# Three gate passes of 48, 32 and 48 sub-tiles instead of four of 32, in a two-layer encoder trunk with product-key experts

## The chip, the cores and the metric

The kernel runs on one core of one Trainium2 chip. A core has TensorE (PE; its weight loads are written PEld), VectorE (DVE), ScalarE (ACT), GpSimd (POOL) and SyncE (SP, which issues the DMAs). The metric is the device time of one execution in microseconds. Before the change it is 2258.52 us, the median of 3 runs (2255.5 to 2259.55).

## The reference

Two layers over 256 tokens of width 1024, all in float32. A layer is a norm, one input projection, sliding-window attention beside an RWKV-7 recurrence, an output projection, then the expert stage, then a gated embedding. The change touches only the expert stage:

```
def _peer(h, wq, keys, u_tab, v_tab):
    q = (h @ wq).reshape(B, S, PEER_HEADS, 2, PEER_HALF)
    sc = jnp.einsum('bshcd,cnd->bshcn', q, keys)          # 128 scores on each of two axes
    top_v, top_i = lax.top_k(sc, 16)
    cand = top_v[..., 0, :, None] + top_v[..., 1, None, :]
    best_v, best_c = lax.top_k(cand.reshape(..., 256), 16)
    expert = i1 * 128 + i2                                 # i1, i2 of the 16 best pairs
    gate = softmax(best_v)
    ...
        u = jnp.take(u_tab, ex, axis=0)
        act = gelu(einsum('thkd,td->thk', u, hx)) * gx
        out = einsum('thk,thkd->td', act, jnp.take(v_tab, ex, axis=0))
```

There are 16384 experts, and a token uses 128 slots of them (8 heads, 16 each). The kernel gathers nothing. It computes the hidden value of every expert for every token, multiplies it with a gate that is zero for unused experts, and multiplies the result with the whole v table.

## The kernel before

Experts are cut by their second index i2 into 128 sub-tiles of 128 experts (i1 is the partition). All products of float32 matrices are done as three products of a high and a low part: ACT copies a tile into `high` (L648), DVE or POOL subtracts it to give `low` (L1083, L435), and TensorE adds high x high, high x low and low x high.

For one sub-tile e there are four kinds of work on TensorE:
- `hidden(e)` (L1624): 24 products of 256 columns, u tile times the tokens; ACT then puts gelu of it into `GA` (L652).
- `spread(g)` (L1636): for a group of 8 tokens, the gates of one pass. For each token it multiplies `hot1` (slots x i1, one-hot) with `hot2` (slots x i2 of the pass; three bfloat16 parts of the gate, each on the one-hot of i2) into one PSUM bank: 3 products of 32 columns a token, 24 a group. The three parts add up in PSUM.
- `spend(s)` (L1647): 12 products of 512 columns, gated activations of sub-tile s times its v tile, summed in PSUM banks 0 to 3.

DVE makes the one-hots of a group in `one_hots` (is_i2 L1146, hot1 L1149, hot2 L1153), after ACT has repeated the slot numbers (`repeat`, L678). DVE multiplies gates into GA in `apply_gates` (L1161), straight from PSUM. ACT and DVE split the gated activations in `split_w` (WH L669, WL L1166).

A pass gives the gates of 32 sub-tiles for all 256 tokens, as 32 groups; there are four passes in a layer. GA holds 64 sub-tiles (`HELD`), so sub-tile 64 + s goes where sub-tile s was. The order of a layer's expert stage is written out by hand and is the same on every engine:
- First part: `hidden` 0 to 39, with POOL making the low parts, while DVE does the top-k.
- Second part: `hidden` 40 to 63 with all 32 spreads of pass 0 between them (DVE makes the low parts from here on).
- Joint part: 64 steps of spread, hidden(64 + s), spend(s): passes 1 and 2.
- Fourth part: 32 steps of spread, spend(64 + s): pass 3.
- Last part: 32 steps of spend(96 + s).

The engines meet only by semaphores. A spread waits for its one-hots (`hots_made`) and for the gates two groups back to be applied (`gated`), since there are two PSUM banks for gates. DVE waits for ACT's repeats (`repeated`) and, before applying, for the spread (`spread_ps`). The tables arrive as slabs of 1 MB of two tiles, through a ring of four, each asked for by SP when DVE or POOL has used the old one.

## Time and profile before

| what | value |
|---|---|
| median of 3 runs | 2258.52 us |
| profiled execution, its own time | 2252.36 us |
| its span | 2250.6 us |
| PE busy | 2162.7 us (96%), 21816 matmuls |
| PEld busy | 1939.7 us (86%) |
| DVE busy | 1588.3 us (71%) |
| ACT busy | 1092.5 us (49%) |
| POOL busy | 336.4 us (15%) |
| granted TensorE clock, mean | 0.987 |
| of the matmuls, L1636 (spread) | 6144 of 128x32, bfloat16 |

The profiled execution is 6.2 us under the median of the runs, so differences are made against its own time and then carried to the median. A busy span of a matmul covers its latency, which overlaps with the next; what one costs in a stream is read from the starts of neighbouring rows. The same is true, to a lesser degree, of DVE: a following instruction often starts before the end of the one before it.

### The profile page before, as it was taken

Reading aid. Unit: us, or ns where it says so; the run is one execution under the profiler, and the core shown is the slowest. Engines: PE = TensorE matmul, PEld = TensorE weight load, DVE = VectorE, ACT = ScalarE, POOL = GpSimd, SP = SyncE. Lnnn points to the kernel's source line nnn. Section 1 sums busy time; section 2 is a strip of 40 time slices with the busy share of each in tenths; the row PEclk is TensorE's granted clock in tenths of the full one; section 3 lists DMA queues with packets and bytes.
Section 4 is the critical chain, followed back from the end, with each engine's and each line's share of the span. In section 5 each row is a group of like instructions: output and inputs, shape, how many; then the busy total and the mean of one; then the engine's idle time right before and its main releaser. Section 6 shows DMA issues by size and latency. Waiting matters only on the chain.

```text
span 2250.6 us, 55219 instructions
## 1 busy us (share of the span) xinstructions
PE 2162.7 (96%) x21816; PEld 1939.7 (86%) x21816; DVE 1588.3 (71%) x3080; ACT 1092.5 (49%) x1881; POOL 336.4 (15%) x166
## 2 busy tenths in 40 slices
PE   8889999999999999999998899999999999999997
PEld 8878999988888888788788789999888888887885
DVE  6645896876666667975576458968766666679755
ACT  5534455444444444444454344554444444444443
POOL 0022696000000000000000237950000000000000
PEclk9999999999999999999999999999999999999999
DMA  6212344434444444445342134443344444444451
GB/s 255 94 41 102 143 171 174 142 131 168 167 164 165 164 165 165 149 168 187 134 149 93 41 125 142 181 167 135 131 168 168 168 168 168 166 153 150 167 200 70
DMA packets 46618, 335.04 MB, mean 149 GB/s; under 512 B 5168, under 2 KB 5296, under 8 KB 6320
## 3 DMA queue, kind: packets, MB, share of 16 engines
q1 hardware_dynamic: 46512, 333.61, 41.2%
q8 instruction: 69, 1.13, 0.2%
q14 instruction: 37, 0.30, 0.0%
HBM read 332.54 MB, written 1.05 MB: 148 GB/s over the span
## 4 chain that ended last, share of the span: by engine, by line
PE 80%; issue 6%; POOL 6%; DVE 5%; ACT 1%; DMA 1%; POOLq 0%; SPq 0%; DVEq 0%; ACTq 0%
PE PS L1647 32%; PE PS L1624 23%; PE PS L1309 8%; PE PS L1636 6%; POOL low L435 5%; PE PS L1325 3%; PE PS L1489 1%; DVE low L1083 1%; PE PS L1527 1%; PE PS L1538 1%; DVE hot L1153 1%; DVE hot L1149 1%; DMA ring<-in_w_slabs 1%; ACT high L459 0%; PE PS L1357 0%
## 5 line engine op out<-in xcount | busy, mean ns | idle before, releaser
L648 ACT CAST high<-ring 128x1024 fp32r<-128x1024 f32 x512 | 535.6, 1048 | 602.1 <-PE PS L1624 443.2
L1624 PE MATMUL PS<-hTh,high 128*128 128x256 f32 x2048 | 594.8, 290 | 13.0 <-ACT GA L652 11.0
L1624 PE MATMUL PS<-hTh,low 128*128 128x256 f32 x2048 | 578.4, 282 | 0.0
L1624 PE MATMUL PS<-hTl,high 128*128 128x256 f32 x2048 | 577.0, 282 | 0.0
L1083 DVE TENSOR_TENSOR low<-ring,high 128x1024 fp32r<-128x1024 f32 x432 | 514.8, 1217 | 0.8 <-ACT high L648 0.6
L1624 PEld LDWEIGHTS PS<-hTh,high 128*128 128x128 f32 x2048 | 387.1, 189 | 17.7 <-ACT GA L652 9.7
L1624 PEld LDWEIGHTS PS<-hTl,high 128*128 128x128 f32 x2048 | 387.6, 189 | 0.0
L1624 PEld LDWEIGHTS PS<-hTh,low 128*128 128x128 f32 x2048 | 387.3, 189 | 0.0
L1647 PE MATMUL PS<-high,WH 128*128 128x512 f32 x1024 | 323.6, 397 | 0.0
L1647 PE MATMUL PS<-low,WH 128*128 128x512 f32 x1024 | 317.9, 392 | 0.0
L1647 PE MATMUL PS<-high,WL 128*128 128x512 f32 x1024 | 316.4, 390 | 0.0
L1146 DVE TENSOR_TENSOR is_i<-iota_half,repeats 128x256 bf16<-128x256 bf16 x256 | 73.8, 288 | 257.1 <-ACT repeats L678 253.0
L395 POOL TENSOR_SCALAR stat<-stat 128x1 f32<-128x1 f32 x14 | 5.1, 367 | 1609.8 <-ACT xn L468 1609.8
L435 POOL TENSOR_TENSOR low<-ring,high 128x1024 fp32r<-128x1024 f32 x80 | 226.4, 2867 | 32.7 <-ACT high L648 32.7
L1647 PEld LDWEIGHTS PS<-high,WL 128*128 128x128 f32 x1024 | 192.2, 188 | 42.9
L1647 PEld LDWEIGHTS PS<-low,WH 128*128 128x128 f32 x1024 | 192.2, 188 | 42.8
L1636 PEld LDWEIGHTS PS<-hot,hot 128*128 128x128 bf16 x6144 | 169.9, 96 | 60.1 <-issue 54.1
L1647 PEld LDWEIGHTS PS<-high,WH 128*128 128x128 f32 x1024 | 178.9, 188 | 26.5
L1636 PE MATMUL PS<-hot,hot 128*128 128x32 bf16 x6144 | 194.0, 177 | 7.6 <-DVE hot L1153 7.6
L669 ACT CAST WH<-GA 128x256 fp32r (+1 forms) x256 | 102.8, 402 | 201.5 <-PE PS L1647 191.0
L1309 PE MATMUL PS<-hTh,high 128*128 128x256 f32 x592 | 172.7, 292 | 2.9 <-DVE hTl L835 2.9
L1149 DVE TENSOR_TENSOR hot<-iota_half,repeats 128x1024 bf16<-128x1024 bf16 x256 | 174.9, 683 | 0.0
(251 smaller groups left out, 2980.1 us busy)
## 6 DMA issues: line engine op xcount, KB each, us to landing
ring<-in_peer_slabs SPq DMA_DIRECT2D x256, 1024.0 KB, 4.8
ring<-in_w_slabs SPq DMA_DIRECT2D x58, 1024.0 KB, 4.8
xres<-in_x SPq DMA_DIRECT2D x2, 512.0 KB, 4.3
out<-obuf SPq DMA_DIRECT2D x2, 512.0 KB, 2.6
cst<-in_consts SPq DMA_DIRECT2D x1, 680.0 KB, 10.1
praw<-in_p_t SPq DMA_DIRECT2D x1, 512.0 KB, 14.8
gfin<-in_g_final SPq DMA_DIRECT2D x1, 512.0 KB, 5.6
vec<-in_vecs SPq DMA_DIRECT2D x1, 356.0 KB, 7.0
```

The source lines that it names most:

```text
L435: pool.tensor_tensor(low[:, b], ring[:, place, half * D:(half + 1) * D], high[:, b].bitcast(F32), ALU.subtract).then_inc(low_pool, 1)
L648: act.copy(high[:, (c0[L] + j) % DEEP], ring[:, place, half * D:(half + 1) * D]).then_inc(part_hi, 1)
L669: act.copy(WH[:, j % 2:j % 2 + 1], GA[:, bass.ds(place, 1)]).then_inc(w_hi, 1)
L1083: dve.tensor_tensor(low[:, b], ring[:, place, half * D:(half + 1) * D], high[:, b].bitcast(F32), ALU.subtract).then_inc(low_dve, 1)
L1146: dve.tensor_tensor(is_i2[:, b].rearrange("p t (a c) -> p t a c", c=REP), iotas[:, QT // REP * chunk:QT // REP * (chunk + 1)].unsqueeze(1) ...
L1149: dve.tensor_tensor(hot1[:, b].rearrange("p t (a c) -> p t a c", c=REP), iotas.unsqueeze(1).broadcast_to([P, GROUP, NSUB // REP, REP]), re ...
L1153: dve.tensor_tensor(hot2[:, b].rearrange("p q t (a c) -> p q t a c", c=REP), is_i2[:, b].rearrange("p t (a c) -> p t a c", c=REP).unsqueez ...
L1309: ins = mm(dst, w[:, b, ks], h[:, k], start=n == 0, stop=n == 3 * KT - 1)
L1325: ins = mm(PS[:, bank0 + 2 * tb + s], h[:, k, tb * P:(tb + 1) * P], w[:, b, s * 512:(s + 1) * 512], start=first and k == 0 and c == 0, sto ...
L1624: ins = mm(PS[:, 6 + j % 2, 0:SEQ], u[:, b, ks], h[:, k], start=n == 0, stop=n == 3 * KT - 1)
L1636: ins = mm(PS[:, 4 + b, t * QT:(t + 1) * QT], hot1[:, b, t], hot2[:, b, part, t], start=part == 0, stop=part == 2)
L1647: ins = mm(PS[:, 2 * tb + s], w[:, j % 2, tb * P:(tb + 1) * P], v[:, b, s * 512:(s + 1) * 512], start=False, stop=False, skip_group_check= ...
```

## The change

Passes are 48, 32 and 48 sub-tiles wide. GA holds 80 sub-tiles. The order is now: `hidden` 0 to 47 with POOL; `hidden` 48 to 79, each followed by one spread of pass 0; 32 steps of spread (pass 1), hidden(80 + s), spend(s); 16 steps of hidden and spend alone; 32 steps of spread (pass 2) and spend(48 + s); 48 steps of spend. In passes 0 and 2 a token still takes three products, of 48 columns. In pass 1 it takes two: one of 64 columns, the first two gate parts side by side, and one of 32 columns, the third part, added onto the second half. The two halves are added by DVE (`sum_gates`, a reduction from PSUM into the new tile `gate_sum`), and `apply_gates` then reads `gate_sum`.

```
-NQ = 4
-QT = NSUB // NQ
-HELD = 2 * QT
+STARTS, WIDTHS = (0, 48, 80), (48, 32, 48)
+NQ, WIDEST = len(WIDTHS), max(WIDTHS)
+HELD = WIDTHS[0] + WIDTHS[1]
+JOINT = NSUB - HELD
-A_FIRST, A_SECOND, A_TOP, A_LOOP = 16, 32, 36, 40
+A_FIRST, A_SECOND, A_TOP, A_LOOP = 16, 32, 44, 48
+        gate_sum = place("gate_sum", 16016, [WIDTHS[1], GROUP])
...
                 def apply_gates(g, group, b, chunk):
+                    start, width = place_of(STARTS[chunk]), WIDTHS[chunk]
+                    acts = GA[:, start:start + width, bass.ds(GROUP * group, GROUP)]
+                    if chunk == 1:
+                        dve.wait_ge(gates_summed, NGROUPS * (L - 1) + 1 + g)
+                        dve.tensor_tensor(acts, acts, gate_sum[:], ALU.mult).then_inc(gated, 1)
+                    else:
+                        dve.wait_ge(spread_ps, g0 + 1 + g)
+                        dve.tensor_tensor(acts, acts, PS[:, 4 + b, 0:GROUP * width].rearrange("p (t i) -> p i t", t=GROUP), ALU.mult).then_inc(gated, 1)
+
+                def sum_gates(g, b):
                     dve.wait_ge(spread_ps, g0 + 1 + g)
-                    acts = GA[:, chunk % 2 * QT:chunk % 2 * QT + QT, bass.ds(GROUP * group, GROUP)]
-                    dve.tensor_tensor(acts, acts, PS[:, 4 + b, 0:GROUP * QT].rearrange("p (t i) -> p i t", t=GROUP), ALU.mult).then_inc(gated, 1)
+                    dve.tensor_reduce(gate_sum[:], PS[:, 4 + b].rearrange("p (t q i) -> p i t q", t=GROUP, q=2), AX.X, ALU.add).then_inc(gates_summed, 1)
...
                 for e in range(A_LOOP, HELD):
                     if e < HELD - 2:
                         split_u(e + 2)
-                    for g in spreads_after(e):
-                        first_chunk(g, g % 2, g == NGROUPS - 1)
+                    first_chunk(e - A_LOOP, e % 2, e == HELD - 1)
...
                 def step(s, j, group, chunk, last=False):
                     one_hots(s + (NGROUPS + 1), (j + 1) % 2, chunk + last)
-                    split_uv(s + 1, j + 1)
+                    split_uv(s + 1, j + 1, 0)
+                    sum_gates(s + NGROUPS, j % 2)
+                    split_uv(s + 1, j + 1, 1)
                     apply_gates(s + NGROUPS, group, j % 2, chunk)
                     split_w(s + 1, s + 1, j + 1)
...
-                def spread(g, b):
+                def spread(g, b, chunk):
+                    width = WIDTHS[chunk]
...
                     for t in range(GROUP):
+                        if chunk == 1:
+                            at = 2 * t * width
+                            mm(PS[:, 4 + b, at:at + 2 * width], hot1[:, b, t], hot2[:, b, 0:2, t, 0:width], start=True, stop=False, skip_group_check=True)
+                            ins = mm(PS[:, 4 + b, at + width:at + 2 * width], hot1[:, b, t], hot2[:, b, 2, t, 0:width], start=False, stop=True, skip_group_check=True)
+                            continue
                         for part in range(3):
-                            ins = mm(PS[:, 4 + b, t * QT:(t + 1) * QT], hot1[:, b, t], hot2[:, b, part, t], start=part == 0, stop=part == 2)
+                            ins = mm(PS[:, 4 + b, t * width:(t + 1) * width], hot1[:, b, t], hot2[:, b, part, t, 0:width], start=part == 0, stop=part == 2)
...
-                with pe.Fori(0, HELD // 4) as i:
+                with pe.Fori(0, NGROUPS // 4) as i:
                     for j in range(4):
-                        spread(4 * i + (j + NGROUPS), j % 2)
+                        spread(4 * i + (j + NGROUPS), j % 2, 1)
                         hidden(4 * i + (j + HELD), j, 2 * j, second=True)
                         spend(4 * i + j, j, 2 * j + 1, low_dve, v0[L] + 2 + 2 * (4 * i + j))
-                with pe.Fori(HELD // 4, (HELD + QT) // 4) as i:
+                with pe.Fori(NGROUPS // 4, JOINT // 4) as i:
                     for j in range(4):
-                        spread(4 * i + (j + NGROUPS), j % 2)
-                        spend(4 * i + j, j, j, low_dve, v0[L] + (HELD + 1) + 4 * i + j)
+                        hidden(4 * i + (j + HELD), j, 2 * j, second=True)
+                        spend(4 * i + j, j, 2 * j + 1, low_dve, v0[L] + 2 + 2 * (4 * i + j))
+                with pe.Fori(JOINT // 4, (JOINT + NGROUPS) // 4) as i:
+                    for j in range(4):
+                        spread(4 * i + (j + 2 * NGROUPS - JOINT), j % 2, 2)
+                        spend(4 * i + j, j, j, low_dve, v0[L] + (JOINT + 1) + 4 * i + j)
```

What stands on TensorE at the start of a joint step (`spread`, then `hidden`), before:

```order
L1636 MATMUL PS<-hot_113,hot_112 128x32 x24
L1612 ISA
L1619 REGISTER_ALU
L1624 MATMUL PS<-hTh,high 128x256
L1624 MATMUL PS<-hTl,high 128x256
```

And now, the first two of the eight tokens:

```order
L1623 MATMUL PS<-hot_114,hot_113 128x64
L1624 MATMUL PS<-hot_114,hot_113 128x32
L1623 MATMUL PS<-hot_114,hot_113 128x64
L1624 MATMUL PS<-hot_114,hot_113 128x32
```

The block of 24 products has become one of 16, alternately of 64 and 32 columns; what follows it is as it was, under other line numbers.

What stands on DVE in a joint step (`step`), with the semaphores waited for, before:

```order
L1146 TENSOR_TENSOR is_i_114<-iota_half,repeats 128x256 [waits repeated]
L1149 TENSOR_TENSOR hot_112<-iota_half,repeats 128x1024
L1153 TENSOR_TENSOR hot_113<-is_i_114,repeats 128x768 [waits is_i2_made]
L1081 ISA
L1083 TENSOR_TENSOR low<-ring,high 128x1024 [waits part_hi]
L1081 REGISTER_ALU
L1083 TENSOR_TENSOR low<-ring,high 128x1024 [waits part_hi]
L1159 REGISTER_ALU
L1161 ISA [waits spread_ps]
L1161 TENSOR_TENSOR GA<-GA,PS 128x32x8
L1165 REGISTER_ALU
L1166 ISA [waits w_hi]
```

And now:

```order
L1125 TENSOR_TENSOR is_i_115<-iota_half,repeats 128x8x32 [waits repeated]
L1128 TENSOR_TENSOR hot_113<-iota_half,repeats 128x1024
L1132 TENSOR_TENSOR hot_114<-is_i_115,repeats 128x24x32 [waits is_i2_made]
L1059 ISA
L1061 TENSOR_TENSOR low<-ring,high 128x1024 [waits part_hi]
L1149 REGISTER_ALU
L1150 TENSOR_REDUCE gate_sum<-PS 128x256 [waits spread_ps]
L1061 TENSOR_TENSOR low<-ring,high 128x1024 [waits part_hi]
L1142 ISA [waits gates_summed]
L1142 TENSOR_TENSOR GA<-GA,gate_sum 128x32x8
L1155 ISA [waits w_hi]
```

The reduction stands between the two subtractions of the slab, the wait for the spread has moved to it, and the one-hots have lost their contiguous shape, since a pass of 32 is now written into tiles laid out for 48.

## Rows read from the trace of the kernel before

**Rows 1.** The page's part 4, the chain that ended last, by engine

```profile
PE 80%; issue 6%; POOL 6%; DVE 5%; ACT 1%; DMA 1%; POOLq 0%; SPq 0%; DVEq 0%; ACTq 0%
```

**Rows 2.** Windows: stretch, us, busy (count) of PE PEld DVE ACT POOL, clock, DMA, GB/s

```profile
389.30:477.10 87.80, 86.12 (x1250) 84.50 (x1249) 73.64 (x141) 40.44 (x76) 0.00 (x0) 1.00 0.39 132
477.10:489.90 12.80, 10.06 (x111) 9.18 (x110) 9.02 (x15) 4.06 (x8) 0.00 (x0) 0.73 0.36 127
480.53:481.20 0.67, 0.67 (x24) 0.67 (x24) 0.67 (x2) 0.40 (x1) 0.00 (x0) 0.50 0.00 0
489.90:886.80 396.90, 396.90 (x3782) 353.86 (x3782) 272.28 (x441) 190.88 (x316) 0.00 (x0) 1.00 0.46 165
886.80:998.00 111.20, 111.20 (x1154) 88.88 (x1154) 100.70 (x190) 54.39 (x96) 0.00 (x0) 1.00 0.42 151
998.00:1085.10 87.10, 87.10 (x386) 72.16 (x385) 51.01 (x64) 43.27 (x63) 0.00 (x0) 1.00 0.55 194
```

**Rows 3.** Timeline of TensorE, a joint step: start us, us, what, count

```profile
565.48 0.77 PE L1636 MATMUL PS<-hot,hot 128*128 128x32 bf16 x24
566.10 0.36 PE L1624 MATMUL PS<-hTh,high 128*128 128x256 f32 x1
569.03 0.63 PE L1647 MATMUL PS<-high,WH 128*128 128x512 f32 x2
```

**Rows 4.** Timeline of DVE, the same step; in brackets the idle time before

```profile
567.12 0.29 DVE L1146 TENSOR_TENSOR is_i<-iota_half,repeats 128x256 bf16<-128x256 bf16 x1 [1.92 <-ACT repeats L678]
567.33 0.68 DVE L1149 TENSOR_TENSOR hot<-iota_half,repeats 128x1024 bf16<-128x1024 bf16 x1
567.93 0.55 DVE L1153 TENSOR_TENSOR hot<-is_i,repeats 128x768 bf16<-128x768 bf16 x1
568.40 2.35 DVE L1083 TENSOR_TENSOR low<-ring,high 128x1024 fp32r<-128x1024 f32 x2
570.67 0.41 DVE L1161 TENSOR_TENSOR GA<-GA,PS 128x256 f32 x1
571.00 0.42 DVE L1166 TENSOR_TENSOR WL<-GA,WH 128x256 fp32r<-128x256 f32 x1
573.42 0.29 DVE L1146 TENSOR_TENSOR is_i<-iota_half,repeats 128x256 bf16<-128x256 bf16 x1 [2.00 <-ACT repeats L678]
```

**Rows 5.** Timeline of TensorE, end of the second part and first joint step

```profile
477.06 1.36 PE L1636 MATMUL PS<-hot,hot 128*128 128x32 bf16 x48
480.53 0.82 PE L1636 MATMUL PS<-hot,hot 128*128 128x32 bf16 x24 [2.10 <-DVE hot L1153]
481.99 0.58 PE L1624 MATMUL PS<-hTh,high 128*128 128x256 f32 x1 [0.64 <-DVE low L1083]
```

**Rows 6.** Timeline of TensorE, two spreads of the second part

```profile
408.96 0.77 PE L1636 MATMUL PS<-hot,hot 128*128 128x32 bf16 x24
412.50 0.77 PE L1636 MATMUL PS<-hot,hot 128*128 128x32 bf16 x24
```

**Rows 7.** Timeline of TensorE, a spread of the fourth part

```profile
928.46 0.77 PE L1636 MATMUL PS<-hot,hot 128*128 128x32 bf16 x24
```

**Rows 8.** Timeline of DVE, the fourth part

```profile
929.38 0.42 DVE L1161 TENSOR_TENSOR GA<-GA,PS 128x256 f32 x1 [0.31 <-PE PS L1636]
932.86 0.42 DVE L1161 TENSOR_TENSOR GA<-GA,PS 128x256 f32 x1 [0.31 <-PE PS L1636]
```

**Rows 9.** Chain of waits, pieces in order of time: start us, us, what

```profile
374.42 14.24 PE PS L1624 x120
...
995.22 89.91 PE PS L1647 x396
```

**Rows 10.** Groups by line: reductions on DVE, shapes, count, busy us, mean ns

```profile
L1124 DVE TENSOR_REDUCE slot<-picked 128x128 f32<-128x2048 f32 x8 | 18.3, 2286 | 0.3
...
L881 DVE TENSOR_REDUCE stat<-lg 128x8 f32<-128x1024 f32 x2 | 2.4, 1220 | 0.1
```

More of the change, by code:

```diff
@@ L213, in hybrid_encoder @@
         GA = place("GA", R, [HELD, SEQ])
[L214 to L219 removed]
+        WH = place("WH", R + 20480, [2, SEQ], F32R)
+        WL = place("WL", R + 20992, [2, SEQ], F32R)
+        hot1 = place("hot1", R + 21504, [2, GROUP, NSUB], BF16)
+        hot2 = place("hot2", R + 22528, [2, 3, GROUP, WIDEST], BF16)
+        is_i2 = place("is_i2", R + 23680, [2, GROUP, WIDEST], BF16)
+        decoded = place("decoded", R + 24064, [5, SEQ], BF16)
         gate_rest = place("gate_rest", R + 22208, [SEQ])
[L221 removed]
+        repeats = place("repeats", R + 24704, [2, 5, GROUP, REP], BF16)
         gate_T = place("gate_T", R + 19968, [SEQ])
@@ L741, in _ @@
+                with act.Fori(0, NGROUPS // RING - 1) as i:
                     for j in range(RING):
-                        step(i, j)
-                for j in range(RING):
-                    step(QT // RING - 1, j)
-                wrap = NGROUPS
-                with act.Fori(QT // RING, HELD // RING - 1) as i:
-                    for j in range(RING):
-                        step(i, j)
-                for s in range(HELD - RING, HELD):
+                        step(i, j, RING * i + j)
@@ L750, in _ @@
+                for s in range(NGROUPS - RING, JOINT - 2):
+                    step(s // RING, s % RING, s, s < NGROUPS)
+                for s in range(JOINT - 2, JOINT):
                     act.wait_ge(w_lo, NSUB * L + 1 + s)
-                    if s < HELD - 2:
-                        split_uv(s // RING, s % RING + 2, 0)
-                    else:
-                        act.wait_ge(part_used, c0[L] + C_UV + 2 * s + 1)
+                    act.wait_ge(part_used, c0[L] + C_UV + 2 * s + 1)
@@ L755, in _ @@
                     gelu(s, s)
[L756 to L771 removed]
+                    if s + 1 == STARTS[1]:
+                        act.wait_ge(gated, NGROUPS * (NQ * L + 2))
@@ L772, in late @@
+                    split_w(s + 1, s + 1, s + 1, C_UV + 2 * s - 1)
+                    for n in ((0,), (1, 2))[s - JOINT + 2]:
+                        split_vv(0, n)
+                def late(n, i, j, place, more=True, again=False):
+                    split_w(n, place, j + 1, C_VV - 1 + n)
                     if more:
@@ L1217, in _ @@
-                for s in range(HELD - RING, HELD):
-                    if s < HELD - 1:
-                        step(s, s % RING, s % QT, 2)
-                    else:
-                        one_hots(s + NGROUPS + 1, 0, 3)
-                        apply_gates(s + NGROUPS, s % QT, 1, 2)
-                        split_w(s + 1, 0, 0)
+                dve.wait_ge(ga_ready, NSUB * L + STARTS[2])
+                with dve.Fori(0, NGROUPS // RING - 1) as i:
+                    for j in range(RING):
+                        step(RING * i + j, j, RING * i + j, 1)
@@ L1224, in _, with last_chunk @@
+                for s in range(NGROUPS - RING, NGROUPS):
+                    step(s, s % RING, s, 1, s == NGROUPS - 1)
+                for s in range(NGROUPS, JOINT - 1):
+                    split_uv(s + 1, s % RING + 1, 0)
+                    split_uv(s + 1, s % RING + 1, 1)
+                    split_w(s + 1, s + 1, s + 1)
+                split_vv(0, 0)
+                split_w(JOINT, JOINT, JOINT)
                 dve.wait_ge(ga_ready, NSUB * (L + 1))
-                def last_chunk(n, j, last=False):
+                def last_chunk(n, j, place, last=False):
@@ L1665, in _ @@
                 ins.then_inc(slot_ps, 1)
-                for e in range(A_TOP, A_LOOP + 4):
-                    hidden(e, e, e, by_dve=e >= POOL_U)
-                    if e in (A_LOOP, A_LOOP + 2):
-                        spread(e // 2 - A_LOOP // 2, e // 2 % 2)
-                with pe.Fori(0, (HELD - A_LOOP - 4) // 4) as i:
-                    for j in range(4):
-                        hidden(4 * i + (j + A_LOOP + 4), j, j, by_dve=True)
-                        spread(6 * i + (2 + 3 * j // 2), 3 * j // 2 % 2)
-                        if j % 2:
-                            spread(6 * i + (2 + 3 * j // 2 + 1), (3 * j // 2 + 1) % 2)
@@ L1678, in _ @@
-                with pe.Fori(0, HELD // 4) as i:
+                for e in range(A_TOP, A_LOOP):
+                    hidden(e, e, e)
+                for e in range(A_LOOP, A_LOOP + 4):
+                    hidden(e, e, e, by_dve=True)
+                    spread(e - A_LOOP, e % 2, 0)
+                with pe.Fori(1, NGROUPS // 4) as i:
+                    for j in range(4):
+                        hidden(4 * i + (j + A_LOOP), j, j, by_dve=True)
+                        spread(4 * i + j, j % 2, 0)
@@ L1691, in _ @@
+                with pe.Fori((JOINT + NGROUPS) // 4, NSUB // 4) as i:
+                    for j in range(4):
+                        spend(4 * i + j, j, j, low_dve, v0[L] + (JOINT + 1) + 4 * i + j)
                 for n in range(4):
```

127 lines of the change are left out of this document (44 added, 83 removed).

## The prediction

> **What bounds the kernel now.** I read the chain of waits first: the reader is to see that PE holds 80% of it [rows 1]. Next the windows, cut at the borders of the parts of layer 0's expert stage: in the joint, the fourth and the last part PE is busy for the whole of the stretch at full granted clock, while DVE is busy for 69% of the first of them (272.28 of 396.90 us) and 91% of the second (100.70 of 111.20 us) [rows 2]. The DMAs are at about half their share. So one TensorE instruction taken out of those parts is time gained, as long as DVE keeps up. Then the timelines of one step, to price single pieces from the starts of rows.
>
> A joint step lasts 6.30 us, from one is_i2 to the next [rows 4]. On PE it is a spread, 0.62 us from its first product to the first of hidden; hidden, 2.93 us to the first of spend; and spend, the remaining 2.75 us [rows 3]. DVE works through its step from 567.12 to about 571.34 and then stands idle for 2.00 us until ACT's repeats arrive [rows 4]; ACT issues those behind its copy of the tile that spend has just freed, so the idle time is PE's lead. A step of the fourth part lasts 3.48 us (929.38 to 932.86), and there DVE has only 0.31 us to spare [rows 8].
>
> **The price of a product.** A block of 48 products of 32 columns takes 0.59 us more than a block of 24 (1.36 against 0.77), so one costs 0.59 us / 24 = 24.6 ns, say 25 ns, with its weight load [rows 3, 5]. At 2.4 GHz 32 columns are 13.3 ns, so more than 11 ns of it are not column time. The same block at half granted clock (0.50, 1.2 GHz) takes 0.82 us [rows 2, 5]; less the latency of about 0.2 us that is 27 ns a product, and 32 columns at 1.2 GHz are 26.7 ns. So at the low clock weight load and overhead hide wholly under the columns, and at the high clock something of 25 ns stands over them. I take it for a floor: 48 columns (20.0 ns) cost 25 ns still, so three products of 48 cost what three of 32 did; 64 columns (26.7 ns) stick out, 28 ns. Bounds: 25 ns for both from below, and from above in proportion to columns, 37.5 and 50 ns. I take the value near the lower end because the half-clock row is the only one of the same instruction at another ratio of column time to the rest.
>
> The Trainium skill, "TensorE: Matmul & The Clock Gate", sections "Wait — 56ns, not 53.3ns?" and "Back-to-back issue gap", states that start-to-start never falls below about 25 ns however small the product and gives about 60 cycles for 1 to 64 columns. The trace agrees at 32 columns (25 ns); no row shows 48 or 64. The same section's formula, columns / 2.4 + 2.5, would make 64 columns 29.2 ns, and the joint block 0.01 us longer than mine.
>
> **The change part by part, for one layer** (layer 0; the other has the same steps).
>
> *Second part.* Before, 87.8 us for 24 hiddens and 30 spreads [rows 2]. Now 8 of the hiddens fall in the first part, where five hiddens in a row take 14.24 us with the last one's latency, 2.84 us each [rows 9]: 22.7 us. POOL makes their low parts, but DVE is done with its top-k by then, as before. Then 32 hiddens with 31 spreads before the border. A hidden with one spread lasts 3.54 us (408.96 to 412.50) [rows 6]: 31 x 3.54 + 2.93 = 112.7 us. DVE has a wider job there. From neighbouring starts [rows 4], bfloat16 work costs 0.21 us for 256 elements, 0.60 for 1024 and 0.47 for 768, so about 0.52 ns an element more; the gate product takes 0.33 us for 256. At 48 wide is_i2 is 0.27, hot2 0.67, the gate product 0.47 us, with hot1 0.60 and one tile's subtraction 1.14 in all 3.15 us, under 3.54: hidden behind PE. After each apply DVE needs 2.7 us to have the next but one's one-hots ready, inside the step too. Sum 135.4 us, +47.6.
>
> *Border to the joint part.* Before, 12.8 us from the last hidden's end to the second joint spread, at a mean granted clock of 0.73 [rows 2]: two spreads at once, then PE idle for 2.10 and 0.64 us, then a whole hidden at half clock [rows 5]. Now one spread stands there and hots for the next are ready, since DVE made them a step earlier. hidden(80) waits for DVE: the gate product starts 0.92 us after the spread's first product (928.46, 929.38) [rows 7, 8], then 0.47 and one subtraction of 1.2 us, 2.65 us in all. With hidden 2.93 and spend 2.86 the second joint spread comes at 8.4 us if the clock holds, and 2.3 us later if it falls as before. PE's idle time shrinks from 2.7 to about 1.5 us but does not go. I take half of that loss: -3.2 (between -4.4 and -2).
>
> *Joint part.* Before, 63 more steps, 396.9 us [rows 2]. The spread is now 8 x (28 + 25) ns = 0.42 us instead of 0.60, so a step is 6.12 us. DVE gains a reduction of 512 elements to 256. The nearest rows are 2286 ns for 2048 elements and 1220 ns for 1024 [rows 10], 1.04 ns an element: 0.68 us; bounds 0.33 us (the pace of the 256-element gate product) and 1.22 us (the row of 1024). All of them fit in the idle 2.00 less the 0.18 us that the step gets shorter. ACT's repeats come as they did; queued behind the reduction are the v subtraction, the gate product and WL, and the earliest reader, the next hidden, needs none of them. So the reduction costs nothing; it would begin to from 1.8 us. 31 steps x 6.12 = 189.7, and 16 steps without a spread, 6.30 - 0.62 = 5.68: 90.9. Sum 280.6, -116.3.
>
> *Fourth part.* 32 steps before and now, at the same 25 ns a product. But DVE's work grows by 0.06 + 0.20 + 0.14 = 0.40 us against 0.31 us of idle time [rows 8], so it falls behind by 0.09 us a step, 2.9 us over 32. PE needs a gated activation late: WL of the next step is done about 1.7 us after the spread's start and read at 3.48 + 0.6, so 2.4 us of lag are free while it builds up. At the end sub-tile 80 needs the last gates of all, and there some of the lag is paid: +1.0 us (0 to 2.9).
>
> *Last part.* 48 spends instead of 32. 396 products take 89.91 us [rows 9], 0.227 us each, 12 a spend: 2.73 us. 16 x 2.73 = +43.7. One slab for two of them was met at 194 GB/s [rows 2] and the steps of 5.68 us ask no more.
>
> Sum a layer: 47.6 - 3.2 - 116.3 + 1.0 + 43.7 = -27.2 us; two layers -54.4. As a check, 32 spreads fewer at 0.62 and 32 shorter by 0.18 make -25.6, and the border -3.2, less the hand-overs. The profiled execution had 2252.4 us, so 2198.0 now (span 2196.2); against the median of 2258.5 that is **2204 us**.
>
> **Rivals.**
> - *Columns add to the overhead.* A float32 product of 256 columns costs 2.84 us / 24 = 118 ns [rows 9], 11.7 ns over its 106.7 ns of columns, and the 32-column product is 11.7 ns over its 13.3. If that sum holds between, 48 columns cost 31.7 ns and 64 cost 38.4. Against it: the half-clock row, where nothing is added, and that the 256-column row is float32, weights and all. It costs 24 x 6.7 = 0.16 us on 64 spreads and 8 x 10.4 = 0.08 us on 32, less the 1.0 of the fourth part, where PE would be slower than DVE: +12.0 a layer, **2228 us**.
> - *Cost in proportion to columns*, 37.5 and 50 ns: +0.30 us on 64 spreads, +0.18 on 32, -1: +23.8 a layer, **2252 us**. The half-clock row speaks for it only at the other clock.
> - *DVE becomes the bound, and the kernel slower.* The one-hots run at 0.52 ns an element, half the float32 pace of 1.04. If tiles written at widths of 48, or 32 in a tile laid out for 48, lose that pace, is_i2 takes 0.48 and hot2 1.28 us, and DVE's step is 3.97 us in the second part (PE 3.54) and 4.31 in the fourth (PE 3.48): 32 x 0.43 + 32 x 0.83 - 2.4 = +37.9, less the 1.0, +36.9 a layer, so 2204 + 74 = **2278 us**. It decides from 0.85 us a step, both parts together. For it: only that the shapes are new. Against: inner runs stay at 8 elements, and 256, 768 and 1024 elements lie on one line.
> - *The third product is not saved*, since the 64-column one costs as two: a case of the second rival.
>
> **How the numbers follow.** Forecast 0.62, added columns 0.23, in proportion 0.05, DVE 0.05, something unseen 0.05 (spread over all outcomes). The likeliest's own range is 2194 to 2213: 25 ns for 64 columns (-3), 27 for 48 (+6), the border's clock (-2 to +2), the fourth part's lag (-2 to +4). Range 2194 to 2232: it takes in the first rival and leaves out the second and third. A measurement here can tell about 0.2% (4.5 us) from no change. Faster by more: the first two cases, most of the unseen and of the proportional one, 0.91; within: 0.04; slower: 0.05.
>
> **What would show it.** Right: joint steps 6.12 us apart, with spread blocks of 0.42 us to the next start, blocks of three times 48 columns still 0.60; steps of 5.68 us after them; DVE idle before is_i2 about 1.1 us in the joint part and never in the fourth; a reduction of 0.6 to 0.7 us; a border of 8.5 to 11 us. Wrong: 48-column blocks of 0.76 us (first rival) or 0.90 (second); DVE without idle time in the second part, PE waiting for hot or WL in the fourth (third).

## The result, and the profile after

The changed kernel takes 2190.93 us, the median of 4 runs (2189.9 to 2195.23), against 2257.01 us for the kernel before beside it (4 runs, 2255.36 to 2259.55): a ratio of 0.971 [0.9693, 0.9727], 66 us less. The forecast was 2204 us, 54.4 us less, with a range from 2194. The direction and the mechanism came out; the gain was forecast 12 us too small, and the time lies 3 us below the range.

The profiled execution of the changed kernel has 2195.23 us and a span of 2193.3 us. First its windows, cut where the parts of layer 0's expert stage meet (first part, second, border, 31 joint steps, 16 steps without a spread, fourth, last), then a window outside that stage. The columns are those of [rows 2].

```profile
265.80:414.20 148.40, 142.50 (x1184) 141.03 (x1183) 104.19 (x214) 80.62 (x114) 129.91 (x47) 1.00 0.50 177
414.20:525.20 111.00, 111.00 (x1490) 109.26 (x1488) 99.02 (x156) 51.94 (x93) 0.00 (x0) 1.00 0.40 142
525.30:533.60 8.30, 6.97 (x79) 6.18 (x78) 7.52 (x11) 3.61 (x7) 0.00 (x0) 1.00 0.39 127
533.60:723.30 189.70, 189.70 (x1614) 169.27 (x1614) 151.97 (x249) 93.90 (x155) 0.00 (x0) 1.00 0.48 171
723.30:813.50 90.20, 90.20 (x577) 81.85 (x575) 44.91 (x51) 42.90 (x65) 0.00 (x0) 1.00 0.51 186
813.50:923.60 110.10, 110.10 (x1153) 89.04 (x1153) 109.63 (x190) 54.21 (x95) 0.00 (x0) 1.00 0.43 153
923.60:1054.20 130.60, 130.60 (x578) 108.17 (x577) 76.64 (x97) 64.97 (x95) 0.00 (x0) 1.00 0.54 194
...
100.00:200.00 100.00, 90.28 (x1923) 76.50 (x1920) 53.91 (x102) 34.90 (x78) 15.54 (x12) 0.91 0.15 55
```

PE is busy for the whole of every stretch but the first and the border. DVE now fills 80% of the joint stretch (151.97 of 189.70 us, before 69%) and 99.6% of the fourth part (109.63 of 110.10), and still PE does not wait there.

A joint step on PE (timeline: start us, us, what), to be held against [rows 3]:

```profile
539.70 0.20 PE L1623 MATMUL PS<-hot,hot 128*128 128x64 bf16 x1
539.74 0.18 PE L1624 MATMUL PS<-hot,hot 128*128 128x32 bf16 x1
...
540.15 0.37 PE L1609 MATMUL PS<-hTh,high 128*128 128x256 f32 x1
...
543.08 0.63 PE L1638 MATMUL PS<-high,WH 128*128 128x512 f32 x2
...
545.82 0.20 PE L1623 MATMUL PS<-hot,hot 128*128 128x64 bf16 x1
```

The spread takes 0.45 us to the start of hidden (0.62 before), hidden 2.93 us to spend, spend 2.74 us: 6.12 us a step. And DVE in the same part, against [rows 4]:

```profile
541.33 0.29 DVE L1125 TENSOR_TENSOR is_i<-iota_half,repeats 128x256 bf16<-128x256 bf16 x1 [1.22 <-ACT repeats L676]
...
542.14 0.55 DVE L1132 TENSOR_TENSOR hot<-is_i,repeats 128x768 bf16<-128x768 bf16 x1
...
543.75 0.68 DVE L1150 TENSOR_REDUCE gate_sum<-PS 128x256 f32<-128x512 f32 x1
...
547.45 0.29 DVE L1125 TENSOR_TENSOR is_i<-iota_half,repeats 128x256 bf16<-128x256 bf16 x1 [1.22 <-ACT repeats L676]
```

The reduction of 0.68 us is there. It was paid out of DVE's idle time before is_i2, of which 1.22 us are left where 2.00 were.

In the chain of waits PE's share goes from 80% [rows 1] to 83%. As before, the chain ends each layer's expert stage with one unbroken piece of PE, which has grown from 396 products [rows 9] to 588. In the list of its pieces (start, us, what):

```profile
920.96 133.38 PE PS L1638 x588
```

Each layer's expert stage, from the first hidden to the last spend, is what the change touches. It took 821.4 and 820.9 us before and takes 788.1 and 788.1 now, 66.1 us less together. The rest of the program took 608.3 us before and 617.1 now, although nothing in it changed: between 100 and 200 us the granted clock was 0.96 in the profile before and 0.91 in this one. Over all profiles of this study that rest lies between 606.8 and 618.5 us, with no order by kernel, so I take the 8.8 us for scatter from run to run. The two layers' stages of one profile agree within 1.6 us, mostly within 0.6, and it is their totals that the experiments below are read by; the medians, over several runs, gain the same 66 us.

### The profile page after: what moved, and what is told of

Read it like the earlier page. It is cut to its first block, busy times and chain, and to the rows that moved or that the text cites. A ratio compares the mean times of both kernels' runs of the same rounds, so it can differ in the third digit from the quotient of the medians.

```text
span 2193.3 us, 50079 instructions
## 1 busy us (share of the span) xinstructions
PE 2113.1 (96%) x19768; PEld 1902.3 (87%) x19768; DVE 1549.5 (71%) x2872; ACT 1070.0 (49%) x1817; POOL 374.4 (17%) x182
## 4 chain that ended last, share of the span: by engine, by line
PE 83%; POOL 6%; issue 6%; DVE 3%; ACT 1%; DMA 1%; POOLq 0%; SPq 0%; ACTq 0%
PE PS L1638 32%; PE PS L1609 26%; PE PS L1294 9%; POOL low L433 6%; PE PS L1627 4%; PE PS L1310 3%; PE PS L1474 1%; PE PS L1523 1%; PE PS L1512 1%; PE PS L1623 1%; PE PS L1445 1%; DMA ring<-in_w_slabs 1%; ACT high L457 1%; PE PS L1342 0%; PE PS L1393 0%
## 5 line engine op out<-in xcount | busy, mean ns | idle before, releaser
L1609 PE MATMUL PS<-hTl,high 128*128 128x256 f32 x2048 | 577.5, 282 | 0.0
L1609 PE MATMUL PS<-hTh,low 128*128 128x256 f32 x2048 | 577.4, 282 | 0.0
L1061 DVE TENSOR_TENSOR low<-ring,high 128x1024 fp32r<-128x1024 f32 x416 | 505.9, 1217 | 26.5 <-ACT high L646 18.5
L433 POOL TENSOR_TENSOR low<-ring,high 128x1024 fp32r<-128x1024 f32 x96 | 264.5, 2787 | 38.7 <-ACT high L646 38.5
L1155 DVE TENSOR_TENSOR WL<-GA,WH 128x256 fp32r<-128x256 f32 x256 | 107.5, 420 | 179.4 <-ACT WH L667 179.4
L1294 PE MATMUL PS<-hTh,low 128*128 128x256 f32 x592 | 168.1, 284 | 0.0
L1294 PE MATMUL PS<-hTl,high 128*128 128x256 f32 x592 | 168.1, 284 | 0.0
L802 DVE TENSOR_TENSOR low<-ring,high 128x1024 fp32r<-128x1024 f32 x86 | 104.4, 1222 | 71.8 <-ACT high L457 71.5
```

The source lines that it names most:

```text
L433: pool.tensor_tensor(low[:, b], ring[:, place, half * D:(half + 1) * D], high[:, b].bitcast(F32), ALU.subtract).then_inc(low_pool, 1)
L802: dve.tensor_tensor(low[:, b], raw(tile.slab, tile.half), high[:, b].bitcast(F32), ALU.subtract).then_inc(low_dve, 1)
L1061: dve.tensor_tensor(low[:, b], ring[:, place, half * D:(half + 1) * D], high[:, b].bitcast(F32), ALU.subtract).then_inc(low_dve, 1)
L1155: dve.tensor_tensor(WL[:, j % 2:j % 2 + 1], GA[:, bass.ds(place, 1)], WH[:, j % 2:j % 2 + 1].bitcast(F32), ALU.subtract).then_inc(w_lo, 1)
L1294: ins = mm(dst, w[:, b, ks], h[:, k], start=n == 0, stop=n == 3 * KT - 1)
L1609: ins = mm(PS[:, 6 + j % 2, 0:SEQ], u[:, b, ks], h[:, k], start=n == 0, stop=n == 3 * KT - 1)
```

## The experiments

Each was compared with the kernel before in the same set of runs. "Stages" are the two layers' expert stages together: before 1642.3, the changed kernel 1576.2.

**1. The widths alone.** The changed kernel, with three products of 32 columns in the joint part again and no reduction.

```
-                    if chunk == 1:
+                    if chunk == 9:
...
-                    sum_gates(s + NGROUPS, j % 2)
```

> The changed kernel, but pass 1 takes three products of 32 columns a token and DVE multiplies straight from PSUM, as in the other passes. Theory (every spread product costs 25 ns on TensorE and all the rest is hidden): the joint steps go back from 6.12 to 6.30 us, so 64 x 0.18 = 11.5 us slower than the changed kernel, about 2202 us; the rest of the gain (some 55 us) is the schedule, 64 spread blocks fewer. Rival (the two-product form brings the gain by freeing PSUM banks or DVE waits, not by its length): more than 20 us slower. Rival (the reduction costs something even now): less than 6 us slower.

Measured: 2201.03 us (ratio 0.9771 [0.9744, 0.9797]), stages 1586.4, so 10.2 more than the changed kernel; 11.5 were expected. In PE's timeline the step is the old one with the spend of the new:

```profile
599.88 0.77 PE L1626 MATMUL PS<-hot,hot 128*128 128x32 bf16 x24
603.43 0.63 PE L1637 MATMUL PS<-high,WH 128*128 128x512 f32 x2
606.16 0.77 PE L1626 MATMUL PS<-hot,hot 128*128 128x32 bf16 x24
```

Starts 6.28 us apart. So 55.9 of the 66.1 us belong to the three wide passes, with the new layout of the tiles (experiment 11), and 10.2 to the two products for three.

**2. The two products alone.** The kernel before, four passes of 32, with two products a token in passes 1 and 2 (64 joint steps a layer).

```
+                        if two:
+                            mm(PS[:, 4 + b, at:at + 2 * QT], hot1[:, b, t], hot2[:, b, 0:2, t], ...)
+                            ins = mm(PS[:, 4 + b, at + QT:at + 2 * QT], hot1[:, b, t], hot2[:, b, 2, t], ...)
```

> The kernel before with four passes of 32, where only passes 1 and 2, all 64 joint steps, take two products a token and DVE's reduction. Theory: joint steps of 6.12 instead of 6.30 us, 128 x 0.18 = 23 us faster than the kernel before, about 2234 us, the border and the fourth part unchanged. Rival (the reduction moves DVE late enough to hold PE when all 64 steps have it): a gain under 12 us.

Measured: 2244.09 us (0.9962 [0.9944, 0.998]), stages 1629.6: 12.7 less than before (9.9 by the medians), not 23. The spread block took 0.45 us as it should; but hidden took 2.96 instead of 2.93 us and spend 2.78 instead of 2.75, with no wait of PE on anything and DVE idle for 1.29 us a step. The step was 6.19 to 6.20 us, not 6.12. The expectation failed, and not by its rival, since no wait holds PE. Why float32 products should run 1% slower here was the open question of experiments 7 to 11.

**3. More reductions.** The changed kernel with the reduction made two and four times over, into the same tile, each waiting for the one before (the diff is that of four).

```
+                    for k in range(4):
...
+                        dve.tensor_reduce(gate_sum[:], PS[:, 4 + b]..., AX.X, ALU.add)...
```

> The changed kernel, with the reduction of pass 1 made twice in every joint step (the second with the same result, each waiting for the one before). Theory (DVE's idle 1.22 us in a joint step covers it): 0.60 us more on DVE for the second and some 0.05 us for the wait are hidden, total within 0.1% of the changed kernel, DVE idle about 0.55 us. Rival (the reduction is on the path): 64 x 0.65 = 42 us slower.

Measured: 2192.7 us (0.9718 [0.9694, 0.9741]), stages 1575.8, no cost. DVE's idle time took it up:

```profile
601.96 0.29 DVE L1125 TENSOR_TENSOR is_i<-iota_half,repeats 128x256 bf16<-128x256 bf16 x1 [0.50 <-ACT repeats L676]
...
604.38 1.41 DVE L1153 TENSOR_REDUCE gate_sum<-PS 128x256 f32<-128x512 f32 x2
```

> The changed kernel, with the reduction of pass 1 made four times in every joint step. Theory (idle 1.22 us is all that covers it): 3 x 0.65 = 1.95 us more on DVE, 0.73 us over the idle time, so joint steps of about 6.85 us and 64 x 0.73 = 47 us slower than the changed kernel, about 2238 us, with DVE never idle in the joint part. Rival (more cover than the idle time shows): under 20 us slower.

Measured: 2239.72 us (0.9936 [0.9915, 0.9958]), stages 1630.4, 54.2 more, where 47 were expected. The four reductions take 2.86 us, not the 0.68 + 1.95 that the expectation put down, and the joint step is 6.98 us instead of 6.85. DVE has no idle time left and PE waits for its WL. DVE, then PE:

```profile
599.59 2.86 DVE L1153 TENSOR_REDUCE gate_sum<-PS 128x256 f32<-128x512 f32 x4
...
604.16 0.28 DVE L1125 TENSOR_TENSOR is_i<-iota_half,repeats 128x256 bf16<-128x256 bf16 x1
```

```profile
604.30 0.73 PE L1641 MATMUL PS<-high,WH 128*128 128x512 f32 x2 [0.57 <-DVE WL L1158]
```

One reduction costs nothing, two cost nothing, four cost 54 us: what counts is whether they fit into the 1.22 us.

**4. Wider products.** The changed kernel, where in the 48-column passes neighbouring tokens' columns are taken two at a time (products of 96 columns, seven of every eight), so that a block keeps its 24 products.

```
+                            n = 2 if t < GROUP - 1 else 1
+                            ins = mm(PS[:, 4 + b, t * width:(t + n) * width], hot1[:, b, t], hot2[:, b, part, t:t + n, 0:width], ...)
```

> The changed kernel, but in passes 0 and 2 the products of tokens 0 to 6 of a group run over 96 columns instead of 48 (the second half is overwritten by the next token, so nothing is left out). Theory floor (a product costs the larger of 25 ns and columns / 2.4 + 2.7 ns, the latter fitted to 54.4 ns for the pair of 64 and 32 columns): 42.7 ns each, 21 x 17.7 = 0.37 us more a block, 128 blocks, 48 us slower, block 0.97 us. Rival (columns add to 11.7 ns): 51.7 ns, 0.56 us more a block, 72 us slower, block 1.16 us.

Measured: 2233.88 us (0.9907 [0.9888, 0.9925]), stages 1622.0, 45.8 more; the theory of a floor (no product under 25 ns) said 48, the rival 72. In PE's timeline a block of 24 now lasts 0.98 us to the next start:

```profile
893.87 1.14 PE L1628 MATMUL PS<-hot,hot 128*128 128x96 bf16 x24
894.85 0.70 PE L1639 MATMUL PS<-high,WH 128*128 128x512 f32 x2
```

The 21 widened products cost (0.98 - 0.62) / 21 = 17 ns more than 48-column ones, 42 ns each; 96 columns at 2.4 GHz are 40 ns. From 48 columns up to 96 the price goes from floor to columns; from 32 to 48 nothing was paid.

**5. The border, one step earlier.** In the changed kernel DVE splits the first joint slab during the last two hiddens of the second part and not after the last spread.

```
+                    else:
+                        split_uv(0, 0, e - HELD + 2)
...
-                split_uv(0, 0, 0)
-                split_uv(0, 0, 1)
```

> The changed kernel, but DVE makes the low parts of the first u and v tile of the joint part one and two steps earlier, where it has nothing to subtract, instead of after the last gates of pass 0. Theory (PE's idle 1.6 us at the border is the wait for that u tile, and the clock holds): the border shrinks from 8.3 to about 6.8 us, 1.5 us a layer, 3 us in all, about 2188 us. Rival (PE then waits for WL or the gates instead): no gain.

Measured: 2183.22 us (0.9684 [0.9659, 0.971]), stages 1573.3, 2.9 less. The border is 6.85 us instead of 8.31, and PE does not wait in it. In the windows (columns as above) and in PE's timeline:

```profile
526.10:533.00 6.90, 6.90 (x79) 6.18 (x78) 5.47 (x10) 3.60 (x7) 0.00 (x0) 1.00 0.46 153
```

```profile
526.13 0.78 PE L1627 MATMUL PS<-hot,hot 128*128 128x48 bf16 x24
526.84 0.20 PE L1623 MATMUL PS<-hot,hot 128*128 128x64 bf16 x1
...
532.98 0.20 PE L1623 MATMUL PS<-hot,hot 128*128 128x64 bf16 x1
```

This is the fastest of the kernels. Only 2.9 us of its distance to the changed kernel are shown to be the border's; the rest is the scatter outside the stages.

**6. The border, later.** The changed kernel with the gates of the last spread but one applied before the next one-hots are made, the order turned round in the last step.

```
+                    if last:
+                        apply_gates(g, g, b, 0)
...
+                    if not last:
+                        apply_gates(g, g, b, 0)
```

> The changed kernel, but at the border DVE makes the first one-hots of pass 1 after the last gates of pass 0 instead of before, so that PE waits for them and then for the u tile, as in the kernel before. Theory (the border's gain of 4.5 us a layer is two parts, the shorter idle time and the clock, which held): idle time grows by some 1.5 us a layer, and if the granted clock then falls to half for the first hidden, 2.3 us more; 3 to 8 us slower in all. Rival (the border's gain came from having one spread instead of two there): under 2 us slower, and no fall of the clock.

Measured: 2189.88 us (0.9713 [0.9698, 0.9728]), the changed kernel's time, where 3 to 8 us more were expected; but stages 1581.1, 4.9 more, and these do show it. PE waits twice, and the clock falls. PE's timeline, then the window:

```profile
522.95 0.78 PE L1630 MATMUL PS<-hot,hot 128*128 128x48 bf16 x24
525.72 0.20 PE L1626 MATMUL PS<-hot,hot 128*128 128x64 bf16 x1 [2.00 <-DVE hot L1132]
...
526.85 0.58 PE L1612 MATMUL PS<-hTh,high 128*128 128x256 f32 x1 [0.54 <-DVE low L1061]
527.23 0.42 PE L1612 MATMUL PS<-hTl,high 128*128 128x256 f32 x1
527.44 0.42 PE L1612 MATMUL PS<-hTh,low 128*128 128x256 f32 x1
```

```profile
522.90:533.90 11.00, 8.47 (x78) 7.58 (x77) 9.33 (x15) 3.60 (x7) 0.00 (x0) 0.84 0.32 104
```

After the first wait, of 2.00 us, the spread still runs at full pace; after another 0.54 us the products start 0.21 us apart (256 columns at 1.2 GHz) and not 0.12. In the changed kernel the one wait of 1.33 us left the clock at 1.00. So of the 2.7 us that this border is longer, 1.2 are waiting and, as the first hidden takes 4.34 us instead of 2.95, 1.4 are clock. The other layer's border repeats it, 11.1 us at a granted clock of 0.85.

**7. Addresses.** The kernel before, with WH, WL, the one-hots and what follows them at the addresses of the changed kernel.

```
-        hot2 = place("hot2", R + 18432, [2, 3, GROUP, QT], BF16)
+        hot2 = place("hot2", R + 22528, [2, 3, GROUP, QT], BF16)
```

> The kernel before with nothing changed but the addresses of WH, WL, hot1, hot2, is_i2, decoded and repeats, which are put where the changed kernel has them. The fourth part's step fell from 3.47 to 3.44 us in the changed kernel though nothing on TensorE got shorter. Theory A (addresses decide how fast the 512-column products run): the fourth part's step is 3.44 us here too, some 2 us less in all. Theory B (what DVE and ACT do at the same moment decides): 3.47 us as before, total within 0.1%.

Measured: 2253.09 us (0.9996 [0.998, 1.0011]), stages 1641.5. WH, WL, hot1 and hot2 have moved by 16 KB in each partition, the others by other distances. The fourth part's step stayed at 3.47 us (PE's timeline):

```profile
906.96 0.77 PE L1636 MATMUL PS<-hot,hot 128*128 128x32 bf16 x24
910.43 0.77 PE L1636 MATMUL PS<-hot,hot 128*128 128x32 bf16 x24
```

**8. Two products, moved.** Experiment 2 with those addresses.

> As e2 (four passes of 32, two products and a reduction in all 64 joint steps), but with WH, WL, hot1, hot2, is_i2, decoded and repeats at the addresses of the changed kernel. In e2 the joint steps were 6.20 us and not 6.12: the spread block was 0.45 us as in the changed kernel, but hidden took 2.96 instead of 2.93 us and spend 2.78 instead of 2.74. Theory A (the addresses, together with the reduction, slow the float32 products): joint steps of 6.12 us here, the expert stages of both layers 1619 us together against 1629.6 in e2. Theory B (addresses don't matter, as the move alone showed without a reduction): steps of 6.20 us again.

Measured: 2245.13 us (0.9949 [0.9932, 0.9966]), stages 1628.4, steps again of 6.19 to 6.20 us. This move does not matter, with two products or with three. It is one move, of a round 16 KB for four of the tiles; no other distance was tried.

**9. DVE's load in the fourth part.** The changed kernel with 32 columns instead of 48 in DVE's one-hots and gate products of the last pass; the gates of the other 16 sub-tiles are left out.

```
+                    start, width = STARTS[chunk], 32 if chunk == 2 else WIDTHS[chunk]
...
+                        n = 32 if chunk == 2 else width
...
```

> The changed kernel, but in pass 2 DVE makes the one-hots of, and applies the gates to, only 32 of the 48 sub-tiles (16 sub-tiles stay ungated; TensorE does all of its products as before). In the changed kernel the fourth part's spend takes 2.82 us, before it took 2.86. Theory C (what DVE does while the products run decides): with DVE's step back at 3.1 us of work and 0.3 us of idle time, spend takes 2.86 us and the fourth part's step 3.47 us, some 2 us more in all. Theory D (something else of the new layout): 2.82 us again.

Measured: 2188.92 us (0.9709 [0.9678, 0.974]), stages 1575.6. DVE has idle time again and PE's step is 3.44 us as it was. DVE, then PE:

```profile
869.90 0.42 DVE L1147 TENSOR_TENSOR GA<-GA,PS 128x256 f32 x1 [0.29 <-PE PS L1629]
```

```profile
865.52 0.78 PE L1629 MATMUL PS<-hot,hot 128*128 128x48 bf16 x24
868.96 0.78 PE L1629 MATMUL PS<-hot,hot 128*128 128x48 bf16 x24
```

How busy DVE is does not decide the pace of the spends either.

**10. The layout of the one-hots.** Experiment 8 with one more edit: the rows of hot2 and is_i2 stand 48 elements apart instead of 32, as in the changed kernel. The same 32 are written and read. The edit also puts the three parts of hot2 768 bytes apart instead of 512, and moves the second buffers; the three were not tried one by one, and "layout" stands for all of them.

```
-        hot2 = place("hot2", R + 22528, [2, 3, GROUP, QT], BF16)
-        is_i2 = place("is_i2", R + 23680, [2, GROUP, QT], BF16)
+        hot2 = place("hot2", R + 22528, [2, 3, GROUP, 48], BF16)
+        is_i2 = place("is_i2", R + 23680, [2, GROUP, 48], BF16)
...
```

> Before's four passes of 32 with two products of 32 per middle token, as in the two earlier runs of that kind, but the one-hots of pass 3 and the gate rows are laid out in memory for 48 columns, as in the changed kernel. Those two runs had joint steps of 6.20 us (float32 products of 2.96 and 2.78 us for a hidden and a spend), the changed kernel 6.12 us (2.93 and 2.74). Theory E, that the layout of the one-hots decides how fast the products beside them run: steps of 6.12 us and products of 2.93 and 2.74. Theory F, that it does not: 6.20 us, 2.96 and 2.78. By theory E the two layers together take about 5 us less than in the earlier run; in the time of the whole kernel, 2241 against 2245, that is about what such a run can scatter.

Measured: 2233.47 us in one run (before 2253.34), stages 1619.6, 8.8 less than in experiment 8 and 22.7 less than before. PE's timelines, experiment 8 first, then this one:

```profile
606.57 0.37 PE L1637 MATMUL PS<-hTh,high 128*128 128x256 f32 x1
609.53 0.64 PE L1665 MATMUL PS<-high,WH 128*128 128x512 f32 x2
612.31 0.20 PE L1650 MATMUL PS<-hot,hot 128*128 128x64 bf16 x1
```

```profile
601.87 0.37 PE L1637 MATMUL PS<-hTh,high 128*128 128x256 f32 x1
604.80 0.63 PE L1665 MATMUL PS<-high,WH 128*128 128x512 f32 x2
607.54 0.20 PE L1650 MATMUL PS<-hot,hot 128*128 128x64 bf16 x1
```

Hidden 2.96 and spend 2.78 us became 2.93 and 2.74. The step is 6.12 us in both layers, and the 23 us that experiment 2 was expected to give are there. It is one run and one profile, and rests on the evenness of its steps. The expectation put the saving over experiment 8 at about 5 us for both layers, which is that of one: in layer 0 the 63 joint steps give 63 x 0.074 = 4.7 us and the fourth part's 31 give 31 x 0.033 = 1.0, and a border of 13.13 against 12.03 us takes 1.1 back.

**11. The layout alone.** The kernel before (at experiment 7's addresses) with that layout and nothing else.

> The kernel before, three products of 32 per token in all four passes, with one edit: the one-hots of pass 3 parts and the gate rows are laid out in memory for 48 columns. In the run just made that layout alone took the two-product joint step from 6.20 to 6.12 us and the spend of the fourth part from 2.86 to 2.82 us. Theory E (the layout makes the float32 products beside it faster wherever they were slow): the fourth part's spend is 2.82 instead of 2.86 us, its step 3.44 instead of 3.47; the joint step, whose products already run at 2.93 and 2.75, stays within 0.01 us of 6.30. The two layers' expert stages together are then 2 to 3.5 us shorter than before's 1642.3, and the whole kernel 0 to 4 us, about what can be told. Theory G (the layout helped only beside the two-product spreads): fourth part 2.86, stages within 0.6 us of before's. The same number says how much of the changed kernel's gain is owed to its layout.

Measured: 2251.84 us (0.9982 [0.9967, 0.9996]), stages 1639.1, 3.2 less than before. The fourth part's step went from 3.47 to 3.44 us (PE's timeline), the joint step, 6.29, is 0.013 shorter, where a stay within 0.01 was expected:

```profile
905.92 0.77 PE L1636 MATMUL PS<-hot,hot 128*128 128x32 bf16 x24
909.36 0.77 PE L1636 MATMUL PS<-hot,hot 128*128 128x32 bf16 x24
```

In layer 0 that is 31 x 0.033 + 63 x 0.013 = 1.8 us, and the rest is a border of 12.03 instead of 12.82 us, a length that scatters between profiles of like kernels (12.0 to 13.1); in layer 1 it went the other way, 13.2 instead of 12.0. So the layout, put in first, gives some 3 of the changed kernel's 66 us. In the kernel with two products it gave 8.8, so its share depends on what stands beside it, and in the changed kernel it was not taken out alone.

The rows tell where in a step the time goes. In the fourth part DVE's hot2 product ends at 907.57 us and its next is_i2 starts at 909.69 in experiment 7; in experiment 11 they stand at 906.57 and 908.66. PE's spread is over by then too. Between them nothing writes or reads hot2 or is_i2, and PE's timeline of that stretch, experiment 7 and then experiment 11, is this:

```profile
908.12 0.63 PE L1647 MATMUL PS<-low,WH 128*128 128x512 f32 x2
...
909.51 0.63 PE L1647 MATMUL PS<-low,WH 128*128 128x512 f32 x2
```

```profile
907.09 0.62 PE L1647 MATMUL PS<-low,WH 128*128 128x512 f32 x2
...
908.45 0.61 PE L1647 MATMUL PS<-low,WH 128*128 128x512 f32 x2
```

Six products take 1.39 us there and 1.36 us here: nearly all of the step's 0.033 us, at a time when the two tiles are left alone. So two accesses to these tiles meeting at the same moment are not what slows these products. The Trainium skill, "SBUF — State Buffer", section "SBUF: two separate sides", states that on the engines' side only the port pair that VectorE and GpSimd share causes contention and that PE waits for nobody. These runs give nothing against that: GpSimd was idle, and the slow products stand where nobody uses the tiles. How the layout reaches them stays open.

## Why the prediction was right, and where it failed

By the prediction's own terms, for layer 0, in us:

| term | forecast | measured |
|---|---|---|
| second part and the hiddens moved ahead of it | +47.6 | 213.8 to 259.4: +45.6 |
| border | -3.2 | 12.8 to 8.3: -4.5 |
| joint part | -116.3 | 396.9 to 280.0: -116.9 |
| fourth part | +1.0 | 111.14 to 110.08: -1.1 |
| last part | +43.7 | 87.1 to 130.6: +43.5 |
| sum | -27.2 | -33.4 |

**The price of a product was right**, and it carried the gain. A block of three times eight products of 48 columns takes 0.62 us to the next start, as 32 columns did: before, and in experiment 1 with the rest of the change held (599.88 to 600.50); the rivals "columns add to the overhead" and "cost in proportion" asked for 0.76 and 0.90. The pair of 64 and 32 columns has starts 0.054 us apart, so at 25 ns for the 32 columns the 64 cost 29 ns; the value taken was 28. The Trainium skill, "TensorE: Matmul & The Clock Gate", section "Back-to-back issue gap", has both a table that puts 1 to 64 columns at about 60 cycles and a formula, columns / 2.4 + 2.5, that gives 29.2 ns for 64: the trace, 29 ns, sides with the formula there. The page means the formula for isolated products and says that at small widths it counts too little once weight loads stand between them; here every product has its weight load, and it holds at 64.

**The joint part was right** to 0.6 us: steps of 6.12 us, and 5.64 instead of 5.68 without a spread, where hidden takes 2.88. **The reduction was right**: 0.68 us, no cost, shown by doubling it. The forecast said that it would begin to cost from 1.8 us on; two reductions (1.41 us) cost nothing and four cost 54 us, which fits.

**The step that failed first is the term "Second part"**: "Before, 87.8 us for 24 hiddens and 30 spreads". That window of [rows 2] holds 1250 products, and 23 hiddens and 29 spreads at 24 each are 1248. The first of the hiddens and spread 0 stand before its left edge: five hiddens of [rows 9] run from 374.42 us to the first spread at 388.5, and they are hiddens 36 to 40. From the same five hiddens the 8 moved ones were priced, so hidden 40 with its spread, 3.54 us, was left out of what before had and counted in what now stands. The term's true form from the same rows is 44.1. That is 3.5 us a layer, 7 of the 12 us, and no experiment was needed to find it: the count in the row's brackets had it. With it the forecast would have been 2197 us, inside the range; the two terms below make up most of what is left. The prediction's own check pointed at it: it came to -25.6 - 3.2 = -28.8 us a layer against the sum's -27.2, and the difference, 1.6 us, was put down to "the hand-overs", which would make a gain smaller but have no price in the rows.

Against the slip stands +1.5 us, between 44.1 and the 45.6 measured. Six of the 31 spreads of the second part hold PE for about 0.75 us to the next start instead of 0.62 (0.77 at 439.06 in the changed kernel), the other pairs of hidden and spread last 3.55 us and not 3.54, and the eight hiddens took 23.1 us, not 22.7. So of the term's net miss, 2.0 us, a part is luck: two errors that went against each other.

**Terms that were mis-sized: the border and the fourth part.** The border's three pieces were as forecast, but the clock held; half of the clock's loss was booked, and none of it came. The border is 8.3 us, below the 8.5 to 11 that were to show the forecast right. PE waited for DVE for 1.33 us:

```profile
525.27 0.78 PE L1627 MATMUL PS<-hot,hot 128*128 128x48 bf16 x24
525.98 0.20 PE L1623 MATMUL PS<-hot,hot 128*128 128x64 bf16 x1
...
527.90 0.38 PE L1609 MATMUL PS<-hTh,high 128*128 128x256 f32 x1 [1.33 <-DVE low L1061]
```

The fourth part was forecast to lose 1.0 us by DVE's growth and gained 1.1. DVE did grow to the full step, without a pause, as the starts of its gate products show, 3.47 us apart:

```profile
867.51 0.54 DVE L1145 TENSOR_TENSOR GA<-GA,PS 128x384 f32 x1
...
870.98 0.54 DVE L1145 TENSOR_TENSOR GA<-GA,PS 128x384 f32 x1
```

It falls behind PE's 3.44 by 0.03 us a step, not 0.09, and all of that fits into the lag that was free. The 0.40 us of added work was right; the slack that it was held against was not. An idle time in brackets counts from the end of the instruction before, and DVE's next instruction can start 0.08 us before that end (567.33 against 567.12 + 0.29 in [rows 4]), so the 0.31 us of [rows 8] were 0.39. The prediction had the better figure at hand: its third rival's 4.31 us, less the 0.82 us that this rival adds, is 3.49. PE's own step is 0.03 us shorter, 1 us a layer, which experiment 11 puts down to the layout. The prediction knew of the layout only as a danger to DVE (its third rival). That rival is dead: hot2 with 1152 elements takes 0.74 us, not more than 0.52 ns an element over the 768, and with 768 in the tile laid out for 48 it takes the old 0.55.

The rest is 0.6 us in the joint part and 0.2 in the last. What was missed is 6.2 us in layer 0 (2.0, 1.3, 2.1, 0.6 and 0.2) and some 5.5 in layer 1, whose border before was 12.0 us and not 12.8: the 12 us.

**The range** was built from prices of products and clocks. It had no room for a slip in counting, and its lower end, 10 us under the forecast, left little beyond those all going one way (7 us). Two of the three did, the border and the fourth part, and the slip was on the same side.

## What to carry to other kernels

A bfloat16 product here costs 25 ns at 32 and at 48 columns and 29 at 64, so work that must issue a fixed number of small products gains by fewer, wider ones until columns stick out. A step of PE of 6 us with 2 us of DVE idle in it takes a DVE instruction of 0.7 us for nothing, and the idle time before the first instruction of DVE's step is the figure to read; where tenths of a microsecond decide, read the slack from starts. When a window is used as "n steps", divide its instruction count by that of a step before its time.

## What the runs showed of the hardware that was not expected

- The pace of float32 products depends on the layout of bfloat16 tiles that other instructions use. With rows 32 elements apart, hidden and spend take 2.96 and 2.78 us beside the two-product spread and spend 2.86 us in the fourth part; with rows 48 apart 2.93, 2.74 and 2.82. Moving them by 16 KB (experiments 7, 8) or lightening DVE (9) did nothing. In the fourth part the slow products stand where nobody writes or reads the two tiles (experiment 11). What carries the effect, the rows' spacing, the 512 bytes between the parts or the place of the second buffers, was not separated, and why the joint steps of the kernel before (2.93, 2.75) nearly escaped it is open too.
- In the five traces with a border looked at, the granted clock fell to the level of 1.2 GHz after waits of PE of 2.10 us (before, [rows 5]) and of 2.00 and 0.54 us with a spread between (experiment 6), and held after one wait of 1.33 us (the changed kernel) or 1.43 (experiment 4) and where there was none (experiment 5).
- The part of the program outside the expert stages, untouched in all kernels, took between 606.8 and 618.5 us. The stage totals of one profile each told a difference of 4.9 us (experiment 6) that the medians of several runs did not.
